# Buffers of a two-layer diffusion block moved to different offsets within 512 bytes (one Trainium2 core)

## What is computed

```python
for l in range(2):
    mx, mc = six modulation vectors each, from silu(c) @ ada_w[l] + ada_b[l]
    hx = modulate(rmsnorm(x, pre_norm[l, 0]), mx[0], mx[1])   # and hc from ctx
    yx, yc = hgrn2_mixer(...) if l == 0 else mamba2_mixer(...)
    x = x + mx[2] * rmsnorm(yx, post_norm[l, 0])              # and ctx, in layer 0
    hx = modulate(rmsnorm(x, pre_norm[l, 1]), mx[3], mx[4])
    a, v = split(hx @ ffn_w_up[l])                            # 1024 -> 2 * 2816
    yx = (silu(conv(a)) * v) @ ffn_w_down[l]                  # 2816 -> 1024
    x = x + mx[5] * rmsnorm(yx, post_norm[l, 1])              # and ctx, in layer 0
return x
```

## Time and profile before

| | |
|---|---|
| runs of the kernel, us | 1620.39, 1621.09, 1618.18 |
| span of the profiled execution, first to last instruction | 1618.0 us |
| time of the profiled execution beside its span | not given apart from the runs; the median stands 2.4 us above the span |
| TensorE (matmul / weight load) busy | 1453.7 us (90%) / 1172.3 us (72%) |
| VectorE / ScalarE / GpSimd busy | 979.9 / 661.6 / 325.8 us |
| mean granted TensorE clock | 0.956 |
| HBM | 181 MB read, 113 GB/s over the span |

### The profile page before, as it was taken

How to read it: one execution, slowest core, us unless ns; L and a number is a source line. 1 busy time by engine, 2 the same in 40 slices (tenths; PEclk the granted TensorE clock), 3 DMA queues, 4 the chain that set the end, 5 groups by cost and what they waited for, 6 DMA issues and landing times.

```text
span 1618.0 us, 22554 instructions
## 1 busy us (share of the span) xinstructions
PE 1453.7 (90%) x8203; PEld 1172.3 (72%) x8203; DVE 979.9 (61%) x1707; ACT 661.6 (41%) x985; POOL 325.8 (20%) x257
## 2 busy tenths in 40 slices
PE   5689999999979879999999978999999878799886
PEld 2456666666656558888888846888888777799886
DVE  1545565656674477761577367666766744884774
ACT  2253444343442343332333233555455534454543
POOL 1100000000002313321232320111112322353432
PEclk9699999999999989999999988999999979899998
DMA  6564654335420212333332321323232124365542
GB/s 218 182 221 142 210 183 138 126 114 170 157 69 10 78 52 78 104 87 95 105 104 68 89 85 35 96 79 98 85 97 86 53 79 130 88 166 159 163 139 92
DMA packets 262336, 183.15 MB, mean 113 GB/s; under 512 B 6738, under 2 KB 236914, under 8 KB 262258
## 3 DMA queue, kind: packets, MB, share of 16 engines
q1 hardware_dynamic: 261714, 180.00, 37.0%
q10 hardware_dynamic: 544, 2.10, 0.3%
HBM read 181.03 MB, written 1.05 MB: 113 GB/s over the span
## 4 chain that ended last, share of the span: by engine, by line
PE 64%; DVE 19%; ACT 8%; issue 6%; DMA 2%; DVEq 1%; SPq 0%; POOL 0%; ACTq 0%; POOLq 0%
PE bank L1789 15%; PE bank L1791 14%; PE bank L1790 14%; DVE conv L1521 4%; DVE st L1363 3%; DVE wl L1207 2%; PE bank L1859 2%; PE bank L1927 2%; PE bank L2273 2%; DVE xT L1274 1%; ACT wh L754 1%; PE bank L1804 1%; PE bank L1805 1%; DMA araw<-in_ada_w 1%; PE bank L1806 1%
## 5 line engine op out<-in xcount | busy, mean ns | idle before, releaser
L1789 PE MATMUL bank<-hh,wh 128*128 128x512 f32 (+1 forms) x1336 | 485.0, 363 | 36.6 <-DVE wl L1207 16.3
L1791 PE MATMUL bank<-hh,wl 128*128 128x512 f32 (+1 forms) x1336 | 473.5, 354 | 0.0
L1790 PE MATMUL bank<-hl,wh 128*128 128x512 f32 (+1 forms) x1336 | 473.1, 354 | 0.0
L1789 PEld LDWEIGHTS bank<-hh,wh 128*128 128x128 f32 x1336 | 257.3, 193 | 83.3 <-DVE wl L1207 20.0
L1790 PEld LDWEIGHTS bank<-hl,wh 128*128 128x128 f32 x1336 | 257.6, 193 | 33.3 <-issue 1.7
L1791 PEld LDWEIGHTS bank<-hh,wl 128*128 128x128 f32 x1336 | 256.9, 192 | 33.9
L1521 DVE SCALAR_TENSOR_TENSOR conv<-bank,pv,conv 128x189 f32<-128x189 f32 (+3 forms) x396 | 172.7, 436 | 70.9 <-ACT conv L986 38.1
L1207 DVE TENSOR_TENSOR wl<-wraw,wh 128x2048 fp32r<-128x2048 f32 (+2 forms) x59 | 128.1, 2171 | 114.6 <-ACT wh L754 114.6
L621 POOL TENSOR_TENSOR wl<-wraw,wh 128x1024 fp32r<-128x1024 f32 (+2 forms) x76 | 141.6, 1864 | 217.9 <-ACT wh L761 217.9
L1220 DVE TENSOR_TENSOR wl<-wraw,wh 128x512 fp32r<-128x512 f32 x118 | 129.7, 1099 | 30.6 <-ACT wh L762 21.7
L1789 PE MATMUL bank<-fh,wh 128*128 128x512 f32 (+1 forms) x352 | 121.2, 344 | 5.8 <-DVE wl L1220 3.2
(11 more groups left out here) (252 smaller groups left out, 2193.0 us busy)
## 6 DMA issues: line engine op xcount, KB each, us to landing
araw<-in_ada_w SPq DMA_DIRECT2D x48, 1024.0 KB, 7.4
wraw<-in_ffn_w_up SPq DMA_DIRECT2D x88, 512.0 KB, 4.6
wraw<-in_mb_w_in SPq DMA_DIRECT2D x48, 512.0 KB, 4.7
wraw<-in_hg_w_in SPq DMA_DIRECT2D x32, 512.0 KB, 5.2
wraw<-in_ffn_w_down SPq DMA_DIRECT2D x32, 384.0 KB, 4.1
wraw<-in_ffn_w_down SPq DMA_DIRECT2D x32, 320.0 KB, 3.6
wraw<-in_mb_w_out SPq DMA_DIRECT2D x16, 512.0 KB, 5.2
wraw<-in_hg_w_in SPq DMA_DIRECT2D x16, 256.0 KB, 3.5
```

Of the source, the lines that this page charges most:

```text
L1789: pe.matmul(dst, W, hi(k), start=(k == 0), stop=False, **skip)
L1790: pe.matmul(dst, W, lo(k), start=False, stop=False, **skip)
L1791: ins = pe.matmul(dst, L, hi(k), start=False, stop=(k == nk - 1), **skip)
```

## The change

It adds five unused buffers as gaps and lengthens the rows of `wh` and `wl`. No instruction is added, removed or reordered; the slices of `wh` and `wl` that are read and written stay the first 2048 elements of each slab, and only addresses differ.

```diff
+GAP_FH = 32
...
     hh = sb(ctx, "hh", [P, KT, T], F32R)
+    sb(ctx, "gap_hl", [P, 8])
     hl = sb(ctx, "hl", [P, KT, T], F32R)
     wraw = sb(ctx, "wraw", [P, 2, 2048])
-    wh = sb(ctx, "wh", [P, 2, 2048], F32R)
-    wl = sb(ctx, "wl", [P, 2, 2048], F32R)
+    sb(ctx, "gap_wh", [P, 120])
+    wh = sb(ctx, "wh", [P, 2, 2052], F32R)
+    sb(ctx, "gap_wl", [P, 8])
+    wl = sb(ctx, "wl", [P, 2, 2096], F32R)
     pv = sb(ctx, "pv", [P, NPROWS])
...
     ff = ExitStack()
+    sb(ff, "gap_fh", [P, GAP_FH])
     fh = sb(ff, "fh", [P, FH[0], T], F32R)
+    sb(ff, "gap_fl", [P, 32])
     fl = sb(ff, "fl", [P, FH[0], T], F32R)
```

## The result

The changed kernel takes 1627.4 us (median of 1626.12, 1627.43 and 1627.90) against 1620.7 for the kernel before, measured beside it. The ratio is 1.0039, with a 95% interval of 1.0021 to 1.0057: slower by 0.4%, clear of the noise. The forecast was 1599, with a range up to 1622, so it missed in sign and in size. The third rival had said 1626. A fourth, disturbed execution of 4977 us counts in no comparison.

The account below looks back on a forecast made before the run. The prediction took TensorE, busy 90% of the span, as the bound. Cheaper matmuls in both mixers and FFNs summed to 21.2 us; 1618.0 - 21.2 = 1596.8, plus 2.4 from span to median, gave 1599, range 1577 to 1622.

Parts of the forecast that it names:

- third rival: Whole kernel: if every distance other than 0 costs 6.7 ns more at 512 columns, +5.5 us, 1626; chance 0.13.
- What bounds the kernel: Whole kernel: TensorE busy 90% of the span at 2.4 GHz; FFN of layer 0 all TensorE, other stages partly.
- the cadence depends on addresses: Split matmuls: each loses 6.7 to 20.0 ns, depending on where the moving operand starts relative to the weights.
- rival 2: Whole kernel: no effect, as something other than addresses fixes the stalls; 1620, chance 0.15.
- The price of a distance: Split matmuls: distance 0 has two stalls of 6.7 ns, any other one; 222.2 ns with 512 columns, 115.6 with 256.
- the picture: Split matmuls: moving stream and slower weight load wait 6.7 ns when they meet within 512 bytes; twice if level, otherwise once.
- The sum over six positions: Three product lines in two slabs: 2 of 6 positions keep distance 0; 8 stalls in 6 matmuls, 8.9 ns each.
- The shares on the path: Part of each saving that counts: FFN layer 0 all, first mixer a half, second 0.9, FFN layer 1 up 0.27.
- The edits priced at nothing: Gaps, longer `wh` and `wl` rows, VectorE offsets and `wraw` at a multiple of 32 bytes: zero cost.
- All stalls go: Split matmuls drop to 216 ns with 512 columns and 113.3 with 256, saving 41.6 us: 1579; chance 0.27.
- Slower: Split matmuls: every distance other than 0 costs 6.7 ns more at 512 columns; +5.5 us, 1626, chance 0.13.
- The chances: Whole kernel: faster 0.72, same 0.15, slower 0.13; the forecast itself 0.45.

Follow-up runs that it names:

- The bursts: Kernels without the model, running 48 matmuls per burst at chosen start places; level float32r took 226.7 ns with 512 columns, 120.0 with 256.
- the map: Model left out; float32r matmuls with weights 0 to 496 bytes ahead of the moving operand: 226.6 to 234.5 ns with 512 columns, 113.3 to 120.0 with 256.
- the triples: Model left out; cycles of three start places as in the product loop, 512 columns: kernel before 226.7 ns, changed kernel 231.1 in both slabs.

## Why the prediction was wrong, point by point

**What bounds the kernel** held. The part that is all TensorE moved with the cadence: 1056 x 4.2 ns up less 528 x 1.6 down make +3.6 us, and from its first to its last product the FFN of layer 0 takes 373.8 us in place of 370.0.

**That the cadence depends on addresses** held, and rival 2 falls with it. The bursts show it with no other engine at work, for the kernel before and for the changed one.

**The price of a distance** is the step that failed. The forecast gave every distance other than 0 one stall of 6.7 ns. With 512 columns, of the 15 places of the map that are not level, 13 cost 228.9 to 234.5; the two that lie 16 bytes to either side of level cost what level does (226.7 and 226.6), and none is cheaper by more than 0.1 ns. The row that the picture couldn't explain, 233.3 for `fh`, was the rule, and the three that it explained weren't evidence for it; the second half of the earlier trace rows, 117.5 and so 10.8 ns over the column time, was no single stall of 6.7 either. Under the triples of the changed kernel the bursts stand at 231.1, the kernel at 231.8. The forecast had 222.2: 8.9 to 9.6 ns too low on 3336 matmuls. With 256 columns it had 115.6; measured 118.2 and 117.8. In FFN up of layer 0 the starts lie 230.8 ns apart, neither at the 216 to 224 that would have borne the forecast out nor at the 233 or more named for the slower case.

**The sum over six positions** was the second fault. It treated each position on its own. One buffer moved costs as much as three, and the same places run at two cadences. With the right prices the sum would have been wrong as well: of the six positions of the changed kernel four stand at places that cost 226.7 alone (0, and 16 bytes) and two at places that cost 233.3 (32 and 224 bytes), which makes 228.9, and the triple takes 231.1. The cadence belongs to the whole sequence and can't be had from its pairs.

**The shares on the path** were usable. With the measured cadences: FFN of layer 0 +3.6; first mixer and its output 960 x 4.2 x 0.5 + 192 x 4.2 = 2.8; second mixer (600 x 4.2 - 576 x 1.6) x 0.9 - 384 x 1.6 = +0.8; FFN of layer 1 (-1056 x 1.6 + 528 x 2.7) x 0.27 = -0.1. Sum 7.1 us, against 7.7 in the spans and 6.7 in the medians. By stages it is looser: the FFN of layer 1 lost about 2 us, where the down products, 1.4 us dearer, seem to count in full and the cheaper up products for nothing, since VectorE sets the end there.

**The edits priced at nothing** held: a slab lands in 4.6 us as before, with `wraw` on a multiple of 32, and the other engines' busy times are the same.

**The rivals.** *All stalls go* falls: 226.6 and 113.3 are the lowest of all float32r bursts with 512 and 256 columns and a load of 128. The floor of 216 in the earlier trace rows is that of a float32 stream, and bfloat16 has it too (215.8). The Trainium skill, page "TensorE: Matmul & The Clock Gate", section "Back-to-back issue gap", gives 216 and 109 ns for the isolated gap at the upper clock. The runs agree in bfloat16 (215.8 and 109.2) and not in float32r. The Trainium skill, page "SBUF — State Buffer", section "Who interferes with whom", says that TensorE never waits on anyone. The runs agree in bfloat16 as far as they go, where the two distances tried make no difference; in float32r the place of the two operands changes the cadence by up to 7.9 ns, whatever the cause. *Slower* was right in time (1626) and nearly in mechanism: it took the one measured distance for the price of them all. It had 231.1 ns for `hh` and 512 columns, and 231.1 is what the bursts gave. That was luck in part: it got there by 4 positions in 6 at 6.7 ns, where the map has only 2 of the 6 dear, and the runs with one buffer moved show that such an addition is not how it works.

**The chances.** 0.13 for the side that came. The trace had two distances at 512 columns, the level one cheap and the other dear. The measured rows spoke for the rival and only the picture for the forecast; the picture should have had the smaller chance.

**Left open.** What the extra columns are. They are whole multiples of 16 at many places (226.7, 233.3, 120.0, 113.3) and not at others (230.0, 116.7), they appear in float32r alone of the three types, and with 512 columns they don't vanish with a short weight load, so the meeting of two read streams is at most part of it. Nor is it known why a stream settles in one rhythm or another, or why triples cost more than their pairs. No run here took the weight load away altogether.

## What to carry to other kernels

Read the cost of a matmul in a stream from the starts of rows 24 or 48 apart, compare it with the column time at the granted clock, and if buffers seem to matter, measure the map of places in a kernel of bursts (0.57 ms for the one here) before moving anything: here it would have said that no place beats level for 512 float32r columns, and that 64 bytes off is better for 256. Put the kernel's own sequence of places into a burst too, since pairs need not add up. If one point of a picture doesn't fit, price by the rows and not by the picture. In this kernel the moving operand and the weights are best kept level, `fh` and `fl` as well: one gap of 64 bytes was worth 0.3%.

## What the runs showed of the hardware that I had not expected

- A float32r stream with weight loads of 128 columns never ran below 226.6 ns for 512 columns and 113.3 for 256, 13.3 and 6.7 ns over the column time at 2.4 GHz, while bfloat16 took 215.8 and 109.2 at both distances tried (256 and 384 bytes).
- The cadence repeats with 256 bytes of distance, and moves by up to 7.9 ns (226.6 to 234.5) within that period with 512 columns and 6.7 (113.3 to 120.0) with 256; level is cheapest for the one and dearest for the other.
- The cadence of a sequence need not be the mean of those of its pairs: 231.7 ns with only `hl` 32 bytes on, where the pairs alone make 228.9.
- A narrower weight load can make the wide stream slower: 226.7, 230.0 and 231.7 ns with 128, 64 and 32 columns of weights, level.
- Some places that aren't level have two or three steady cadences (113.3 and 117.8; 230.0, 231.1 and 233.3) behind different bursts; the level place with a load of 128 columns had one in every trial.
